# Tile 0's expert sum as products with diagonals of the gates, a new order behind it, and an earlier load of half of v

## The chip, the cores and the metric

The kernel runs on one core of one Trainium2 chip. What counts is the device time of one execution in microseconds (us); for the kernel before it is the median of three runs. A measurement of this kernel repeats within about 0.1%.

## What is computed

Two transformer-like blocks run one behind the other on 512 tokens of width 1024. The change lies at the seam: the end of the first block's mixture of experts, the two norms, and the first product of the second block. Cut to this:

```python
gates = jax.nn.softmax(top_val, axis=-1)              # 4 of 32 experts for each token
y_rows = lax.map(expert_block, (x_blocks, block_e)).reshape(n_rows, d)
y_rows = y_rows * row_gate[:, None]
y = jnp.zeros((n_tok, d), h.dtype).at[row_tok].add(y_rows)
x = x + g2[:, None, :] * y                            # end of the MoE
x = _rmsnorm(x, final_g)                              # end of the first block
h = rms_norm(x, g_norm[l]) * (1.0 + scale[:, None, :]) + shift[:, None, :]
proj = h @ w_in[l]                                    # q, k, v, gates ...
```

So each token's result is the sum of four rows of y_rows, each times a gate; then come a residual, a norm, a second norm, and the product with v's weights.

## The kernel before

Each engine has its own program, and semaphores order them. Tokens lie in TT = 4 tiles of P = 128; the width is KT = 8 slabs of 128. x_t and h_t hold x and h with the width on the partitions.

**The experts.** In NP = 33 passes TensorE multiplies gathered rows by expert weights, which SyncE (SP) loads into 16 slots; the results go by keep_y to y_sb and by store_quarter to y_rows in HBM, in four stores for each pass. Of the last pass ScalarE issues two stores and SP two (lines 476 to 478). Then each engine reads how many spare blocks there are (none in these runs) and passes an empty loop; in it TensorE executes keep_on(1, 3) three times. keep_on(count, bank) (L607 to L610) is filler: `count` products of the identity with a constant of 128x512, whose result nobody reads.

**The gathers.** GpSimd waits until all stores have landed, then issues 16 indirect gathers (L2467) of 128 rows of 4 KB each: parts[:, 4t + k] is the k-th expert's row of each token of tile t. The four of tile 0 signal one by one ("first parts 0" to "first parts 3"), those of tiles 1 to 3 together for each tile.

**Tile by tile.** For tile t VectorE makes add_part(t, 0) to (t, 3): acc = sum of gate times part (L2168 and L2170, 128x1024). TensorE has put the experts' second bias into two PSUM banks (second_bias, L1037), and turn_sum(t) (L1045) adds the transposed sum, 8 matmuls with the identity as moving operand; each signals after its first and its second half ("sum turned"). VectorE adds it to x_t, residual(t) (L2181, 8 operations in two halves), ScalarE squares both halves (L1519), TensorE adds the squares up in norm_sums(t) (L1053), ScalarE takes the root (L1523, for tile 0 behind a load of its function table), VectorE the reciprocal (tile_scale, L2187), TensorE spreads it over the partitions (spread_scale, L1059), VectorE scales (tile_scaled, L2193, 8 operations) and ScalarE shifts (L1528, 8 operations), which gives h. Then v_rows(t, i) (L1071) multiplies h of the tile by half i of v's weights: 8 matmuls of 512 columns. Half i lies in ring[4i + 4 : 4i + 8]; load_v(0) is issued behind the last use of those slots as expert weights, load_v(1) behind the gather of part 3 of tile 0 (L500, L501; the DMA itself is L472). ScalarE keeps the results (keep_v_rows, L1532).

**What sets the order.** It is written out by hand in each engine's program. TensorE: second_bias(0), (1), (2), keep_on(6, 0), turn_sum(0), keep_on(2, 0), norm_sums(0), keep_on(2, 0), spread_scale(0), turn_sum(1), v_rows(0, 0), norm_sums(1), v_rows(0, 1), spread_scale(1), turn_sum(2), v_rows(1, 0), norm_sums(2), v_rows(1, 1) and so on. VectorE: the parts of tile 0, residual(0), three parts of tile 1, tile_scale(0), the fourth, tile_scaled(0), residual(1), tile 2's four parts, three of tile 3, tile_scale(1), the fourth, tile_scaled(1), residual(2), and so on. A matmul of these types stands in the trace as two records, so v_rows has 16, and turn_sum too.

Behind v come 40 pairs of weight slabs (pair_begun, pair_ended, L1112), with attention and a recurrent layer between them.

## Time and profile before

| | us |
|---|---|
| median of 3 runs (lowest, highest) | 1996.19 (1994.83, 1996.49) |
| the profiled execution | 1998.96 |
| its span, first to last instruction | 1997.7 |
| TensorE matmuls busy | 1937.8 |
| VectorE busy | 836.2 |
| ScalarE busy | 424.7 |
| GpSimd busy | 240.0 |

Mean granted TensorE clock: 0.987 of full speed. Times in rows count from the first instruction. PE is TensorE, PEld its weight loads, DVE VectorE, ACT ScalarE, POOL GpSimd; SPq, ACTq and POOLq are DMA issues of SyncE, ScalarE and GpSimd. L12 is line 12 of the kernel. A row of the timeline gives start, duration, engine, line, operation, output and inputs, shape, count, and in brackets the idle time of that engine before it with what ended it; "remote" there means that the profile knows the moment of the release but no instruction to put it to. Rows that are equal and adjacent are merged, with the count behind the x. The ends of matmuls are modelled. "1.00" in a clock column is 2.4 GHz, "0.50" 1.2 GHz.

### The profile page before, as it was taken

To read this page: it belongs to the slowest core of one execution; us is meant where nothing else is said; L and a number is where in the kernel's file an instruction comes from. 1 tells how busy PE (TensorE), PEld (TensorE's weight loads), DVE (VectorE), ACT (ScalarE), POOL (GpSimd) and SP (SyncE) were. 2 spreads that over 40 slices of the span, in tenths; PEclk is the share of its full clock that TensorE was granted. 3 is DMA by queue.
4 is the path that set the end of the run, shared out by engine and by line. 5 is a ranking of instruction groups with operands and counts; after the bars stand their busy time and mean duration, and the time that the engine had idled before them with its cause. 6 is when DMAs were issued, how large, how long until landed. Compare 5 with 4: busy or idle time off the path is not lost.

```text
span 1997.7 us, 38345 instructions
## 1 busy us (share of the span) xinstructions
PE 1937.8 (97%) x16481; PEld 1079.1 (54%) x16481; DVE 836.2 (42%) x1530; ACT 424.7 (21%) x914; POOL 240.0 (12%) x173
## 2 busy tenths in 40 slices
PE   8999998999999999999999999989999999999998
PEld 4455544433434434343443433345588888888887
DVE  5989875211121211121120211105458678654465
ACT  3223512210111110011010111102233443431102
POOL 0000000000000000000000000002244334360011
PEclk8999998999999999999999999998999999999999
DMA  8475796999799999999999999975112112122221
GB/s 339 139 282 195 286 335 268 420 419 366 319 421 419 420 420 419 421 419 420 419 419 420 418 420 416 419 295 225 63 68 89 67 67 89 66 85 85 85 85 64
DMA packets 103419, 553.94 MB, mean 277 GB/s; under 512 B 14224, under 2 KB 25488, under 8 KB 48336
## 3 DMA queue, kind: packets, MB, share of 16 engines
q1 hardware_dynamic: 81344, 516.84, 64.1%
q10 hardware_dynamic: 14848, 17.82, 2.7%
q0 software_dynamic: 7056, 16.79, 2.3%
q8 instruction: 133, 2.18, 0.4%
q14 instruction: 38, 0.31, 0.0%
HBM read 532.91 MB, written 26.35 MB: 280 GB/s over the span
## 4 chain that ended last, share of the span: by engine, by line
PE 72%; DMA 13%; SPq 10%; DVE 3%; issue 2%; ACT 1%; another core or an unknown queue 0%; ACTq 0%; DVEq 0%
PE psum L1112 24%; PE psum L926 19%; DMA arena<-in_w 9%; SPq L467 9%; PE psum L934 9%; PE psum L597 7%; PE psum L1071 3%; DMA ring<-in_w 2%; DMA arena<-in_mod_slabs 1%; PE psum L919 1%; PE psum L1199 1%; PE psum L1218 1%; PE psum L942 1%; PE psum L906 1%; PE psum L781 1%
## 5 line engine op out<-in xcount | busy, mean ns | idle before, releaser
L926 PE MATMUL psum<-arena,ring 128*32 128x512 f32 x4096 | 452.7, 596 | 11.3 <-DMA arena<-in_w 10.8
L926 PEld LDWEIGHTS psum<-arena,ring 128*32 128x32 f32 x4096 | 134.3, 110 | 310.1 <-issue 307.1
L2114 DVE TENSOR_SCALAR h_t<-psum 128x512 f32<-128x512 f32 (+2 forms) x33 | 27.9, 845 | 572.5 <-PE psum L926 572.5
L934 PE MATMUL psum<-arena,h_t 128*32 128x256 f32 x3840 | 217.9, 380 | 4.2 <-DMA arena<-in_w 3.3
L1458 ACT ACTIVATE ring<-psum,mods,gain 128x64 f32<-128x64 f32 (+2 forms) x264 | 85.6, 429 | 607.5 <-PE psum L906 607.5
L934 PEld LDWEIGHTS psum<-arena,h_t 128*32 128x32 f32 x3840 | 120.7, 110 | 101.1 <-issue 18.7
L2435 POOL DMA_INDIRECT ring<-h_rows,row_i x33 | 35.5, 1075 | 1144.0 <-PE psum L906 834.9
L1112 PE MATMUL psum<-ring 128*128 128x256 f32 x768 | 171.1, 379 | 0.0
L1112 PEld LDWEIGHTS psum<-ring 128*128 128x128 f32 x768 | 145.9, 190 | 20.1 <-issue 0.3
L1112 PE MATMUL psum<-h_t,ring 128*128 128x256 f32 x672 | 154.3, 379 | 0.2 <-ACT arena L1532 0.2
L926 PE MATMUL psum<-ring 128*32 128x512 f32 x1344 | 148.8, 593 | 5.5 <-DMA ring<-in_w 5.4
L1112 PEld LDWEIGHTS psum<-h_t,ring 128*128 128x128 f32 x672 | 126.4, 190 | 23.8 <-issue 7.7
L597 PE MATMUL psum<-h_t,ring 128*128 128x512 f32 x256 | 116.8, 611 | 2.5 <-ACT h_t L1278 2.5
L1112 PE MATMUL psum<-arena,ring 128*128 128x256 f32 x544 | 119.1, 379 | 0.0
L1112 PEld LDWEIGHTS psum<-arena,ring 128*128 128x128 f32 x544 | 103.3, 190 | 14.2 <-DVE arena L2268 0.2
L926 PEld LDWEIGHTS psum<-ring 128*32 128x32 f32 x1344 | 44.4, 110 | 103.4 <-issue 103.4
L934 PE MATMUL psum<-ring,h_t 128*32 128x256 f32 x1600 | 90.9, 380 | 3.8 <-DMA ring<-in_w 3.1
L2128 DVE COPY h_t<-psum 128x512 f32<-128x512 f32 (+2 forms) x33 | 27.9, 845 | 154.9 <-PE psum L942 154.9
L597 PEld LDWEIGHTS psum<-h_t,ring 128*128 128x128 f32 x256 | 48.7, 195 | 62.9 <-issue 61.8
L1466 ACT ACTIVATE work<-psum 128x512 f32<-128x512 f32 (+2 forms) x33 | 23.8, 720 | 240.8 <-PE psum L934 240.8
L934 PEld LDWEIGHTS psum<-ring,h_t 128*32 128x32 f32 x1600 | 50.2, 110 | 43.8 <-issue 7.8
L1112 PE MATMUL psum<-work,ring 128*128 128x256 f32 x256 | 60.7, 380 | 1.7 <-DVE work L2268 1.7
(480 smaller groups left out, 2132.6 us busy)
## 6 DMA issues: line engine op xcount, KB each, us to landing
arena<-in_w SPq DMA_DIRECT2D x288, 1024.0 KB, 30.9
ring<-in_w SPq DMA_DIRECT2D x96, 1024.0 KB
ring<-in_pairs SPq DMA_DIRECT2D x40, 1024.0 KB, 4.8
ring<-in_dot_slabs SPq DMA_DIRECT2D x40, 512.0 KB, 5.9
ring<-in_mod_slabs SPq DMA_DIRECT2D x6, 2048.0 KB, 9.2
ring<-in_proj_slabs SPq DMA_DIRECT2D x24, 512.0 KB, 4.4
y_rows<-arena SPq DMA_DIRECT2D x3, 3584.0 KB, 25.0
y_rows<-work ACTq DMA_DIRECT2D x70, 64.0 KB, 7.7
```

The costliest lines, as they stand in the source:

```text
L467: sp.dma_start(slot[s], source).then_inc(sem(f"weights {s} loaded"), 16)
L597: mm = pe.matmul(bank, ring[:, n % 4, k, :], src[:, k, :], start=(k == 0), stop=(k == KT - 1))
L781: mm = pe.matmul(bank, w_glu[:, m, k, :], proj[:, k, :], start=(k == 0), stop=(k == 3))
L926: mm = pe.matmul(psum[32 * j:32 * j + 32, g, :], x_e[:, c * tokens + g * TG:c * tokens + g * TG + TG], slot[s][:, j * S:(j + 1) * S], star ...
L934: mm = pe.matmul(psum[32 * j:32 * j + 32, 6 + g // 2, (g % 2) * 256:(g % 2) * 256 + 256], h_e[:, g * 256 + half * P + 32 * c:g * 256 + hal ...
L1071: mm = pe.matmul(psum[:, 4 + i, :], h_t[:, k, t * P:(t + 1) * P], ring[:, 4 * i + 4:4 * i + 8, k, :], start=(k == 0), stop=(k == KT - 1))
L1112: mm = pe.matmul(out, stationary[:, k, :], moving[:, k, :], start=(start and k == 0), stop=(k == 3), skip_group_check=True)
L1458: act.activation(x_e[:, k * tokens:(k + 1) * tokens], psum[:, 4 + k // 4, (k % 4) * tokens:(k % 4 + 1) * tokens], ACT.Identity, bias=mods[ ...
L1466: act.activation(dst[:, 0:256 * groups], src[:, 0:256 * groups], ACT.Copy).then_inc(sem("y kept"), 1)
L2114: dve.tensor_scalar(gate, psum[:, 0:groups, 0:256], LIMIT, None, ALU.min).then_inc(sem("gate clipped"), 1)
L2128: dve.tensor_copy(h_e[:, 0:256 * groups], src[:, 0:256 * groups]).then_inc(sem("h_e kept"), 1)
L2435: pool.indirect_dma_start(out=x_g[n][0:rows, :], out_offset=None, in_=h_rows, in_offset=bass.IndirectOffsetOnAxis(ap=index, axis=0), bound ...
```

## The change

Tile 0's sum is made on TensorE: VectorE writes four diagonal matrices, identity times the gates of one expert rank, into by_gate (the space of x_g[1], which is free then), and turn_parts multiplies each part by its diagonal as soon as it has been gathered, 32 matmuls that add up in PSUM. The ten filler products around it go. turn_sum(1) moves behind v_rows(0, 0); norm_sums(1) moves into the middle of v_rows(0, 1); VectorE makes tile 1's four parts behind tile_scaled(0); ScalarE keeps v_rows(0, 0) ahead of the squares of tile 1. SP issues load_v(1) directly behind its two stores of the last pass, without the wait for part 3.

```diff
@@ -294,6 +294,7 @@
+        by_gate = x_g[1][:, 0:TOPK * P].rearrange("p (k n) -> p k n", k=TOPK)
@@ -476,6 +477,7 @@
                 store_quarter(sp, NP - 1, j)
+            load_v(1)
@@ -497,8 +499,6 @@
-            sp.wait_ge(sem("first parts 3 gathered"), 16)
-            load_v(1)
@@ -1038,9 +1038,19 @@
+            def turn_parts():
+                a = SUM_AT[0]
+                pe.wait_ge(sem("gates laid out"), TOPK)
+                for part in range(TOPK):
+                    pe.wait_ge(sem(f"first parts {part} gathered"), 16)
+                    for k in range(KT):
+                        mm = pe.matmul(psum[:, a + k // 4, (k % 4) * P:(k % 4 + 1) * P], parts[:, part, k * P:(k + 1) * P], by_gate[:, part, :], start=False, stop=(part == TOPK - 1), skip_group_check=True)
+                        if part == TOPK - 1 and k % 4 == 3:
+                            mm.then_inc(sem("sum turned"), 1)
             def turn_sum(t):
-                pe.wait_ge(sem("parts summed"), t + 1)
+                pe.wait_ge(sem("parts summed"), t)
@@ -1061,7 +1071,7 @@
-            def v_rows(t, i):
+            def v_rows(t, i, between=None):
@@ -1069,6 +1079,8 @@
+                    if between and k == 3:
+                        between()
@@ -1077,16 +1089,12 @@
             second_bias(2)
-            keep_on(6, 0)
-            turn_sum(0)
-            keep_on(2, 0)
+            turn_parts()
             norm_sums(0)
-            keep_on(2, 0)
             spread_scale(0)
+            v_rows(0, 0)
             turn_sum(1)
-            v_rows(0, 0)
-            norm_sums(1)
-            v_rows(0, 1)
+            v_rows(0, 1, lambda: norm_sums(1))
             spread_scale(1)
@@ -1538,8 +1546,8 @@
+            keep_v_rows(0, 0)
             tile_squares(1)
-            keep_v_rows(0, 0)
             tile_root(1)
@@ -2160,9 +2168,7 @@
-                if t == 0:
-                    dve.wait_ge(sem(f"first parts {k} gathered"), 16)
-                elif k == 0:
+                if k == 0:
                     dve.wait_ge(sem(f"parts {t} gathered"), 16 * TOPK)
@@ -2192,14 +2198,14 @@
+            dve.wait_ge(sem("x turned"), NP)
             for k in range(TOPK):
-                add_part(0, k)
+                dve.tensor_scalar(by_gate[:, k, :], identity, gates[:, 0, k:k + 1], None, ALU.mult).then_inc(sem("gates laid out"), 1)
             residual(0)
-            for k in range(3):
+            tile_scale(0)
+            tile_scaled(0)
+            for k in range(TOPK):
                 add_part(1, k)
-            tile_scale(0)
-            add_part(1, 3)
-            tile_scaled(0)
             residual(1)
```

## Rows read from the trace of the kernel before

**Rows 1.** The page's first part: busy us, share of the span, instructions.
```profile
PE 1937.8 (97%) x16481; PEld 1079.1 (54%) x16481; DVE 836.2 (42%) x1530; ACT 424.7 (21%) x914; POOL 240.0 (12%) x173
```

**Rows 2.** The chain that ended last, 1330 to 1450 us: start, duration, what.
```profile
1369.27 3.78 PE psum L1045 x16
1373.05 8.14 PE psum L1071 x16
...
1382.87 6.97 PE psum L1071 x16
...
1389.95 1.79 PE psum L1045 x16
...
1398.61 1.68 PE psum L1053 x16
...
1427.59 13.99 PE psum L1071 x32
```

**Rows 3.** Windows: busy us (instructions) of each engine, granted clock, DMA share, GB/s.
```profile
1345.00:1350.00 5.00, 5.00 (x51) 4.22 (x51) 0.82 (x1) 0.00 (x0) 3.78 (x5) 1.00 0.72 225
...
1360.00:1365.00 5.00, 3.27 (x14) 2.66 (x15) 2.99 (x6) 1.91 (x2) 3.78 (x5) 0.68 1.02 415
...
1375.00:1380.00 5.00, 5.00 (x12) 2.13 (x11) 4.89 (x5) 0.00 (x0) 0.00 (x0) 0.95 0.45 184
```

**Rows 4.** DMA queues (packets, MB, share): 1356 to 1357; 1360 to 1365; 1350 to 1355.
```profile
q1 hardware_dynamic: 9, 0.04, 12.7%
...
q1 hardware_dynamic: 265, 1.08, 52.6%
q0 software_dynamic: 276, 1.00, 49.5%
...
q0 software_dynamic: 450, 1.63, 93.8%
```

**Rows 5.** Timeline, from the last stores of y to tile 0's turned sum.
```profile
1339.89 1.81 SPq L350 DMA_DIRECT2D y_rows<-work  x2
...
1344.60 0.95 POOL L2467 DMA_INDIRECT arena<-y_rows,slot_i  x1 [115.15 <-DMA y_rows<-work]
...
1354.47 0.41 SPq L472 DMA_DIRECT2D ring<-in_v_slabs  x1
1354.54 1.28 DVE L2170 SCALAR_TENSOR_TENSOR arena<-arena,cols 128x1024 f32<-128x1024 f32 x1 [0.27 <-issue]
...
1355.88 2.05 PE L1045 MATMUL psum<-consts,arena 128*128 128x128 f32 x16 [1.42 <-issue]
```

**Rows 6.** Timeline, from there to the scale of tile 0.
```profile
1357.77 1.89 PE L610 MATMUL psum<-consts 128*128 128x512 f32 x4
...
1360.33 1.13 DVE L2181 SCALAR_TENSOR_TENSOR x_t<-psum,mods,x_t 128x128 f32<-128x128 f32 x4 [1.75 <-remote]
...
1362.14 1.28 ACT L1523 ACT_TABLE_LOAD   x1
...
1362.17 1.86 PE L1053 MATMUL psum<-par,h_t 128*128 128x2 f32 x8 [1.74 <-ACT h_t L1519]
...
1363.90 3.76 PE L610 MATMUL psum<-consts 128*128 128x512 f32 x4
...
1367.50 0.26 ACT L1523 ACTIVATE par<-psum,consts 128x1 f32<-128x1 f32 x1 [4.08 <-remote]
...
1368.08 0.48 PE L1059 MATMUL psum<-consts,par 128*128 128x128 f32 x1 [0.42 <-DVE par L2187]
```

**Rows 7.** Timeline: releases by matmuls of tiles 1 and 2, and the one of L886.
```profile
1373.09 1.13 DVE L2181 SCALAR_TENSOR_TENSOR x_t<-psum,mods,x_t 128x128 f32<-128x128 f32 x4 [0.58 <-PE psum L1045]
...
1400.32 0.26 ACT L1523 ACTIVATE par<-psum,consts 128x1 f32<-128x1 f32 x1 [1.08 <-PE psum L1053]
...
317.44 0.23 DVE L2027 COPY work<-psum 128x64 f32<-128x64 f32 x1 [0.86 <-PE psum L886]
```

**Rows 8.** Timeline: three multiply-adds of tile 2.
```profile
1374.91 3.92 DVE L2170 SCALAR_TENSOR_TENSOR arena<-arena,cols 128x1024 f32<-128x1024 f32 x3
```

## The prediction

> **What bounds the kernel now.** I read the page first: TensorE is busy 97% of the span [rows 1], so a change pays only where it takes time out of TensorE's own row or closes one of its holes. The diff touches one stretch, between the last expert product (1339 us) and the first paired product (1442 us). The second view is the chain of waits in that stretch [rows 2]. From 1369.27 us on the chain is TensorE without a hole worth naming: turn_sum(1), v_rows(0, 0), norm_sums(1), v_rows(0, 1) and so on to v_rows(3, 1), whose last group ends at 1441.6 us. What follows (40 pairs of slabs) is on TensorE too. So whatever brings v_rows(0, 0) forward from 1373.05 us arrives at the end of the kernel, less what is put into the dense part behind it.
>
> Before 1369 us the chain is the path of tile 0, and TensorE waits in it. The timeline [rows 5, 6] shows: the last stores of y are issued at 1339.9 to 1341.7, the first gather at 1344.60, and the fourth part of tile 0 is there at about 1354.4 (the second half of v's slabs, which waits for it, is issued at 1354.47). VectorE multiplies in part 3 (1.28 us), TensorE turns the sum (2.05 us), then come residual, squares, norm_sums, root, spread, scaling. Two steps of this take far longer than their instructions. The second half of the sum has left TensorE at 1357.93, yet the residual that waits for it starts at 1360.33; norm_sums ends at 1364.03, yet the root that waits for it starts at 1367.50. The profile names no releaser ("remote") for either. Both times the matmuls directly behind the one that signals are those of keep_on, the filler products: 1357.77 to 1359.66 and 1363.90 to 1367.66 [rows 6].
>
> The windows [rows 3] add two facts. The granted clock falls within 1360 to 1365 (mean 0.68), in spite of the filler, from 2.4 to 1.2 GHz; in 1375 to 1380 the mean is 0.95, so it is back at about 1375.5. And the DMA engines are full in the window at 1360 (share 1.02), but not in the one at 1345 (0.72).
>
> **The change part by part.** *The v load moved up.* On SP's queue it goes from behind the wait for part 3 (1354.47) to directly behind the two stores of y, so to 1341.75 [rows 5]. Nothing waits behind it on SP but scalar work; ScalarE's and SP's stores are already issued. Its first packets came about 2.0 us after its issue (9 packets in 1356 to 1357) [rows 4], so now at 1343.75, which is 0.85 us ahead of the first gather; that gather waits for the stores to land, and SP's stores stand ahead of the load in its queue: I take no cost there, and 0.5 us as the upper end. Its 2.1 MB run alone until the gathers' packets start (1346.2, 1.6 us behind their issue), which, at the 415 GB/s of full engines [rows 3] is 1.0 MB. The other 1.1 MB share the engines: while both queues ran, v's had 1.08 MB and the gathers 1.00 MB in 5 us [rows 4]. That is 5 us to 1351.2, with 0.95 MB of gathers done. Four parts are 2.1 MB; the rest goes at the rate of the gathers alone, 1.63 MB in 5 us, so 3.5 us, and about 1.1 us lie between last byte and release as before (four parts' bytes were over at 1353.2 by the same rates, the release was at 1354.4): 1355.8 instead of 1354.4. Cost 1.4 us at the head (bounds: 0.5, if the idle engines take nearly all of v; 2.5, if v goes wholly first). The gathers of tiles 1 to 3 gain, as v no longer runs beside them; they are off the path. The old place covered nothing: v_rows(0, 1) starts at 1382.9, and is now reached at about 1375, 24 us behind v's last byte.
>
> *The sum of tile 0 on TensorE.* Four multiply-adds on VectorE go (of them 1.28 us behind the last part count). Four products with diagonals of the gates come (128x128; the nearest row has four such operations in 1.13 us [rows 6]; VectorE does them while it waits for the first part, and would have to be 1 us late for them to show; nothing). TensorE does 32 matmuls instead of 8: 1.79 to 2.05 us per part [rows 2, 5]. The parts come every 1.3 to 2 us, so it falls behind: 1350.5, 1353.1, 1355.0 and, for part 3, 1356.9 as start. That is 1.0 us later than turn_sum(0) starts now (1355.88). So this edit alone wins nothing at the head; it pays through DVE's queue later.
>
> *keep_on gone.* I expect the two late releases to go with it. Against 1.75 and 4.08 us of idle "remote" [rows 6] stand releases of the same kinds where no filler follows: the second half of the residual of tile 1 starts at 1373.09, 0.04 us after turn_sum(1)'s last record, and the root of tile 2 at 1400.32, as soon behind norm_sums(2) [rows 2, 7]. One row speaks against: the matmul of L886 is followed by keep_on(4, 3), and VectorE, which waited for it, starts at 317.44, with L886 named as releaser [rows 7]. I cannot name the mechanism, so both ends stay: nothing is left of the stalls, or all of it.
>
> *Tile 0 from the start of part 3's products.* First half of the residual ends at +2.25, second at +3.4 (1.13 us each); square and start of the table load +0.7; table load 1.28 (norm_sums's second half, 0.95 to 1.86 us, lies beside it); root 0.3; its end to the end of spread_scale 0.8; scaling and shift of the first slab 0.8 (the first waits 0.3 behind spread_scale, each takes 0.3 to 0.4) [rows 6]. Together 7.5 us: v_rows(0, 0) starts at 1364.4, against 1373.05: **minus 8.7 us**. The Trainium skill (ScalarE: Activation LUTs, What ACT_TABLE_LOAD costs) adds a drain of about 1.38 us to each switch of tables; by it the sum would be 1.4 us worse. The trace shows the load taking 1.28 us and nothing that must be a drain, so I leave it out.
>
> *Order behind it.* turn_sum(1) now stands behind v_rows(0, 0): **plus 1.8** [rows 2]. VectorE sums tile 1 behind tile_scaled(0), 7 us after that begins, which v_rows(0, 0) (6.9 us, more at the lower clock) hides; if it ran at full clock at once, 0.3 us would show. norm_sums(1) between k = 3 and 4 is free: its squares are ready 1.5 us before. keep_v_rows(0, 0) ahead of tile_squares(1) is free as well.
>
> *A new wait.* tile_scale(1) still stands behind add_part(2, 0 to 3) and add_part(3, 0 to 2). From the start of turn_sum(1): residual(1) ends at +3.3, tile 2 costs 0.75 + 3.92 [rows 8], three parts of tile 3 3.4, the reciprocal 0.1: +11.5. TensorE arrives at spread_scale(1) at 1.79 + 6.97 + 1.68 = +10.45 [rows 2]. **Plus 1.1**; then h of tile 1 is 0.1 late for v_rows(1, 0). Now this is covered, since the sums run while TensorE is still in v_rows(0, 0).
>
> *Clock.* Before, v_rows(0, 0) took 8.14 us instead of 6.87: 1.27 lost behind its start [rows 2]. Dense work began at 1369.27 and the clock returned at 1375.5, 6.2 us later [rows 2, 3]. Now the thin stretch ahead is as long (about 1358.8 to 1364.4), so the clock is again low at the start of v_rows(0, 0). If it stays so for the same 6.2 us, half of that, 3.1, is lost (plus 1.8); if for half as long, 1.6 (plus 0.3). The nearer row is the first, but dense work now begins with v_rows itself and not with a turn_sum; I take 5.2 us: 2.6 lost, **plus 1.3**.
>
> Sum: -8.7 + 1.8 + 1.2 + 1.3 = **-4.4 us**. The profiled execution (1998.96, its span 1997.7) would come to 1994.6; its median of runs is 1996.19, so 1991.8. The forecast's own range, from the terms' bounds (head -0.9 to +1.1, clock -1.0 to +0.5, the wait at spread_scale(1) to either side by 0.5), is 1990.2 to 1993.6.
>
> **Rivals.**
> A, *late releases stay* (slower): if they belong to the full DMA engines of that stretch and not to the filler, the root is again 6.1 us late (1367.50 against 1355.88 + 5.5). -4.4 + 6.1 = +1.7: 1997.9. For it: the engines are full [rows 3] and the keep_on behind L886 is harmless [rows 7]. Against: turn_sum(1) at 1369 to 1373 releases on time [rows 7], while the gathers still run. It is slower than before once more than 4.4 of the 6.1 us remain.
> B, *the clock falls inside the part products*: between second_bias and part 0, and between parts, TensorE has nothing to do, where six fillers stood. At the lower clock 16 records take 3.78 us [rows 2] instead of 2.05 [rows 5]; two parts slow cost about 3 us: 1994.8. Against: the window 1345 to 1350 stays at 1.00 [rows 3], though its first 4 us hold only second_bias. The Trainium skill (TensorE: Matmul & The Clock Gate, Part 1) has an idle array fall to half clock, which speaks against taking the filler out. By that the trace agrees only in part: the clock fell with the filler in place too [rows 3].
> C, *the v load hurts the head more*: stores of y late and v ahead of all gathers, +1.6 us: 1993.4.
> D, *more is won*: v fills only idle time and the clock returns early: 1989.8.
>
> **How the numbers follow.** Forecast 0.56, A 0.14, B 0.11, C 0.10, D 0.09. A measurement of this kernel tells about 0.2% (4.0 us) from no change, so "faster" is below 1992.2: D and rather more than half of the forecast's range, 0.44; "slower" (over 2000.2) needs A with B or C (0.03) or something that no row shows (0.04), 0.07; the rest, 0.49, is "same". The range 1989.2 to 1997.5 leaves out the worst half of A and the best of D.
>
> **What would show it.** Right: turn_parts's last products start near 1357; residual(0) and root(0) are released within 0.1 us of their matmuls; v_rows(0, 0) starts near 1364.4; one idle place of about 1 us ahead of spread_scale(1), ended by VectorE; low clock until 1367 to 1371; v's packets over by 1351.5. Wrong: "remote" waits at those two lines again (A), the granted clock at 0.50 before 1358 (B), the first gather later than 1344.8 or part 3 later than 1356.5 (C). It would also be wrong if tile 2's or 3's parts held VectorE.

## The result and the profile after

The changed kernel takes 2004.58 us (median of 11 runs, 2001.69 to 2009.9). The kernel before, in 11 runs beside it, takes 1996.87 (1991.22 to 2002.37). The ratio is 1.0036, 95% interval 1.0024 to 1.0048: about 7 us slower (7.7 by the medians), where 4.4 us faster was forecast. The profiled execution (2001.69, span 2000.4) is the shortest of the eleven, so the traces understate the difference: its span is only 2.7 us longer than that of before.

| | us |
|---|---|
| the profiled execution | 2001.69 |
| its span | 2000.4 |
| TensorE matmuls busy | 1935.2 |
| VectorE busy | 832.6 |
| mean granted clock | 0.986 |

TensorE has 2.6 us less to do than in [rows 1], so the time went into holes:

```profile
PE 1935.2 (97%) x16509; PEld 1084.0 (54%) x16509; DVE 832.6 (42%) x1530; ACT 424.8 (21%) x914; POOL 238.5 (12%) x173
```

The moment of the first gather differs from execution to execution, from 1336.35 to 1344.60 us over all traces of this study. What it depends on isn't known. So from here on stages are counted from the issue of the first gather; in before that is 1344.60 [rows 5], in after 1338.97. The timeline of after, the columns as in [rows 5]; L1037 is second_bias, L1047 turn_parts, L2187 residual, L1063 norm_sums, L1531 the root, L1069 spread_scale, L1081 v_rows, L1055 turn_sum, L2193 tile_scale:

```profile
1338.97 0.95 POOL L2473 DMA_INDIRECT arena<-y_rows,slot_i  x1 [115.14 <-DMA y_rows<-work]
1340.17 7.17 PE L1037 MATMUL psum<-work,ring 32*128 32x128 f32 x48
...
1347.27 5.51 PE L1047 MATMUL psum<-ring,arena 128*128 128x128 f32 x28
...
1354.53 0.27 PE L1047 MATMUL psum<-ring,arena 128*128 128x128 f32 x1 [0.93 <-issue]
...
1355.93 0.49 PE L1047 MATMUL psum<-ring,arena 128*128 128x128 f32 x2 [1.12 <-issue]
...
1358.05 0.27 PE L1047 MATMUL psum<-ring,arena 128*128 128x128 f32 x1 [1.64 <-issue]
...
1360.88 0.37 PE L1047 MATMUL psum<-ring,arena 128*128 128x128 f32 x1 [1.54 <-issue]
1361.58 4.98 PE L1047 MATMUL psum<-ring,arena 128*128 128x128 f32 x27 [0.33 <-issue]
1365.70 2.16 DVE L2187 SCALAR_TENSOR_TENSOR x_t<-psum,mods,x_t 128x128 f32<-128x128 f32 x8 [35.78 <-PE psum L1047]
...
1370.30 0.26 ACT L1531 ACTIVATE par<-psum,consts 128x1 f32<-128x1 f32 x1 [0.47 <-PE psum L1063]
...
1372.25 8.79 PE L1081 MATMUL psum<-ring,h_t 128*128 128x512 f32 x16 [0.96 <-ACT h_t L1536]
...
1380.87 1.95 PE L1055 MATMUL psum<-consts,arena 128*128 128x128 f32 x16
...
1392.08 0.16 DVE L2193 RECIPROCAL par<-par 128x1 f32<-128x1 f32 x1
...
1392.30 0.32 PE L1069 MATMUL psum<-consts,par 128*128 128x128 f32 x1 [0.82 <-DVE par L2193]
```

Three things stand in it. The bias takes 7.17 us. The 64 records of the products fall apart: between 1352.8 and 1361.6 TensorE executes nine of them and is idle between them with no wait, only "issue" behind the arrow, seven holes of 0.31 to 1.64 us, 6.3 us in all. And on this trace the waits by which the two late releases of before were seen (1.75 and 4.08 us "remote" [rows 6]) are gone: residual and root each start 0.2 us or less behind the matmul that signals.

The windows of after (columns as in [rows 3]):

```profile
1345.00:1350.00 5.00, 5.00 (x30) 4.78 (x28) 0.00 (x0) 0.00 (x0) 3.75 (x4) 0.50 1.03 409
1350.00:1355.00 5.00, 3.56 (x21) 3.19 (x20) 0.00 (x0) 0.00 (x0) 3.74 (x4) 0.83 1.02 407
1355.00:1360.00 5.00, 1.32 (x4) 1.06 (x5) 0.00 (x0) 0.00 (x0) 2.81 (x3) 0.86 1.03 410
1360.00:1365.00 5.00, 3.79 (x18) 3.71 (x18) 0.00 (x0) 0.00 (x0) 0.00 (x0) 0.50 0.72 288
```

The clock is at 1.2 GHz while the bias and the first products run, then at 2.4 GHz through most of the holes, then at 1.2 GHz again. In the window at 1355 TensorE is busy 1.32 of 5 us beside full DMA engines. It can't be waiting for a part: the packets of tile 0's four gathers were over 10.0 us behind the first gather, the holes lie at 13.8 to 22.6 us, and six of the seven stand inside a part, three of these between the two records of one matmul, where the program has no wait. Nor is late loading of instructions to be seen: the instruction queue (q8) moved one packet at 1.8 us and one at 10.8 us, 1.0 us each, as in e6 below (2.0 and 11.0), which has no holes.

One thing is missing from this trace. Behind a gather's rows come 16 packets of 4 bytes, which update its semaphore (256 such packets for the sixteen gathers in every trace, and 256 updates in e6), and from the updates the profile tells when it landed. In its list of DMA issues the gathers of e6 have a median time from issue to landing, those of after none (e6 first, then after):

```profile
arena<-y_rows,slot_i POOLq DMA_INDIRECT x16, 7.3
```

```profile
arena<-y_rows,slot_i POOLq DMA_INDIRECT x16
```

All packets are there in both traces, but many updates are not in that of after: from 4 to 22 us behind the first gather it has 219 such packets and 48 updates, from 22 us on 37 and 38. That stretch takes in the holes and begins some 10 us ahead of them. So "issue" and "remote" are weak words there: the profile can't name a releaser that wasn't recorded.

The stages of all traces, in us behind the first gather. Each time is that at which a record starts: "bias" and "products" (turn_sum(0) or turn_parts) are first to last record, "end of v" is the last record of v_rows(3, 1), 556.6 to 557.2 us ahead of the end of the span in every trace. A record's own length comes on top: the products of e6 start their last record at 17.6 and end at 17.9 us.

| trace | kernel before in the same measurement | bias | products | v_rows(0, 0) | end of v | from v_rows(0, 0) to the end of v |
|---|---|---|---|---|---|---|
| before | | 0.6-4.2 | 11.3-13.1 | 28.2 | 96.4 | 68.1 |
| after | 1996.87 | 1.2-8.0 | 8.3-27.3 | 33.3 | 104.8 | 71.5 |
| e5, before | 1991.14 | 2.4-9.1 | 17.5-19.1 | 27.3 | 94.2 | 66.8 |
| e10, before | 1989.59 | 2.0-8.7 | 17.1-18.8 | 27.0 | 93.8 | 66.8 |
| e6, after | 1991.14 | 0.8-7.6 | 7.9-17.6 | 23.6 | 95.0 | 71.5 |
| e9, after | 1989.59 | 2.2-9.0 | 9.3-19.1 | 25.0 | 96.6 | 71.6 |
| e15, after | 1989.98 | 0.3-6.4 | 7.1-15.7 | 21.0 | 93.9 | 72.9 |
| e17, after | 1996.95 | 0.2-6.6 | 7.5-24.7 | 30.9 | 102.6 | 71.7 |
| e1 | 1991.03 | 1.7-5.6 | 12.6-14.4 | 22.9 | 89.7 | 66.8 |
| e2, late load | 1991.03 | 2.0-8.7 | 9.1-18.9 | 24.7 | 96.3 | 71.6 |
| e4, other queue | 1991.03 | 0.2-5.2 | 8.2-18.2 | 23.6 | 95.1 | 71.5 |
| e12, entry filler | 1989.98 | 0.8-10.8 | 11.1-20.9 | 26.8 | 98.4 | 71.6 |
| e14, products, entry filler | 1989.98 | 0.8-12.0 | 12.3-21.1 | 29.3 | 96.1 | 66.8 |
| e13 | 1989.98 | 0.6-7.1 | 15.0-16.7 | 24.9 | 91.7 | 66.8 |
| e16, order alone | 1996.95 | 0.6-6.9 | 14.3-15.9 | 31.2 | 102.7 | 71.5 |
| e8, products alone | 1991.14 | 1.2-7.9 | 15.8-22.8 | 31.0 | 97.8 | 66.8 |
| e7, with filler | 1991.14 | 1.7-8.4 | 16.2-23.2 | 29.8 | 99.6 | 69.8 |
| e3, held | 1991.03 | 1.1-7.8 | 8.2-17.6 | 22.9 | 96.6 | 73.7 |
| e11, held | 1989.59 | 1.7-5.4 | 7.3-16.0 | 22.0 | 98.3 | 76.3 |
| e18, held | 1997.24 | 2.0-8.8 | 9.1-18.8 | 24.8 | 100.9 | 76.1 |

The last column goes by the order of instructions: 66.8 us in the old one (68.1 in before, whose clock is low at v_rows(0, 0)), 71.5 to 71.7 in the new one (72.9 in e15, 69.8 in e7, where the clock is full at v_rows(0, 0)), more where gathers are held. The products' column is where the chips differ. The measurements fell on several chips, and the second column sorts them: on three of them (e1 to e15) the kernel before takes 1989.6 to 1991.1 us, on two others (e16 and e17; e18) and in the first measurement, whose chip isn't known, 1996.9 to 1997.2. I call the latter the 1997 chips. So the kernel's time repeats within 0.1% on one chip (1991.03 and 1989.59 on that of e1 and of e9), but chips differ by 0.4%. The traces of the 1997 chips alone lack updates: in the 50 us behind the first gather they hold 124 (after), 125 (e17), 143 (e16), 192 (e18) and 195 (before) by DMA, all others 301 to 304.

### The profile page after: what moved, and what is told of

Its sections match the earlier page's. It is cut to its first block, busy times and chain, and to the rows that moved or that the text cites. A ratio compares the mean times of both kernels' runs of the same rounds, so it can differ in the third digit from the quotient of the medians.

```text
span 2000.4 us, 38398 instructions
## 1 busy us (share of the span) xinstructions
PE 1935.2 (97%) x16509; PEld 1084.0 (54%) x16509; DVE 832.6 (42%) x1530; ACT 424.8 (21%) x914; POOL 238.5 (12%) x173
## 4 chain that ended last, share of the span: by engine, by line
PE 68%; DMA 14%; SPq 13%; DVE 3%; issue 2%; ACT 1%; ACTq 0%; DVEq 0%
PE psum L1120 24%; PE psum L926 16%; SPq L468 12%; DMA arena<-in_w 9%; PE psum L597 7%; PE psum L934 7%; DMA ring<-in_w 3%; PE psum L1081 3%; DMA arena<-in_mod_slabs 1%; PE psum L1207 1%; PE psum L1226 1%; PE psum L919 1%; PE psum L781 1%; PE psum L1212 1%; PE psum L1047 1%
## 5 line engine op out<-in xcount | busy, mean ns | idle before, releaser
L926 PE MATMUL psum<-arena,ring 128*32 128x512 f32 x4096 | 450.4, 593 | 12.8 <-DMA arena<-in_w 12.2
L934 PEld LDWEIGHTS psum<-arena,h_t 128*32 128x32 f32 x3840 | 120.8, 110 | 100.8 <-issue 17.9
## 6 DMA issues: line engine op xcount, KB each, us to landing
arena<-in_w SPq DMA_DIRECT2D x288, 1024.0 KB, 30.9
ring<-in_w SPq DMA_DIRECT2D x96, 1024.0 KB, 30.9
```

The lines of the kernel that those rows point to most:

```text
L926: mm = pe.matmul(psum[32 * j:32 * j + 32, g, :], x_e[:, c * tokens + g * TG:c * tokens + g * TG + TG], slot[s][:, j * S:(j + 1) * S], star ...
L934: mm = pe.matmul(psum[32 * j:32 * j + 32, 6 + g // 2, (g % 2) * 256:(g % 2) * 256 + 256], h_e[:, g * 256 + half * P + 32 * c:g * 256 + hal ...
```

## The experiments

**e1 to e4: early load alone; products with a late load; held gathers; another queue.** The question: which part costs, and do the gathers of tiles 1 to 3 disturb TensorE? e1 is the kernel before with load_v(1) behind the stores. e2 is the changed kernel with load_v(1) at its old place. The edit of e1, and of e3 in the changed kernel:

```diff
+            load_v(1)
...
-            sp.wait_ge(sem("first parts 3 gathered"), 16)
-            load_v(1)
```

```diff
             for n in range(TT * TOPK):
+                if n == TOPK:
+                    pool.wait_ge(sem("sum turned"), 2)
```

e4 leaves out the gathers of tiles 1 to 3 and lets SyncE load consecutive rows of the same size in their place, behind the same waits for the stores. Its output isn't the reference's; it is there for its trace:

```diff
...
+            for n in range(TOPK, TT * TOPK):
+                sp.dma_start(parts[:, n, :], y_rows[n * P:(n + 1) * P, :]).then_inc(sem(f"parts {n // TOPK} gathered"), 16)
...
-            for n in range(TT * TOPK):
+            for n in range(TOPK):
```

> The kernel before with one edit: load_v(1) directly behind the last stores of y. Measure: from the issue of the first gather to the start of v_rows(0, 0) it was 28.45 us in the kernel before and 33.3 us in the changed one. Theory V (the early load of v is what hurts): about half or more of the 4.8 us appears here, 31 to 33 us, and the time is 3 us or more above that of before. Theory G (TensorE completes its instructions slowly while the gathers' traffic runs, and the change puts 32 matmuls of tile 0's path into that stretch): the load costs the head 0.6 to 1.4 us and frees the later gathers, so 28 to 30 us and a time within 2 us of before.

> The changed kernel with load_v(1) back in its old place behind the fourth part. Theory V: the stretch from first gather to v_rows(0, 0) falls to 28 to 29 us, and the time to that of before or below. Theory G: the products still run beside the gathers, TensorE shows gaps of 0.7 to 1.9 us between matmuls that wait for nothing, and the stretch stays at 31 to 35 us, the time 5 to 9 us above before.

> The changed kernel, but GpSimd issues the gathers of tiles 1 to 3 only when tile 0's sum has been turned (semaphore sum turned at 2). Theory G: the gaps inside the 32 products go, part 3's products end about 2 us after part 3 lands, some 12 us after the first gather instead of 27.6, and v_rows(0, 0) starts 18 to 20 us after the first gather; then tile 1's parts are late (4 gathers, about 8 us after the sum) but hidden or nearly so by v_rows(0, 0). The time is 4 to 10 us below the changed kernel. Theory C (the low clock, since the filler is gone, is what makes the products slow): the gaps stay, the stretch stays over 28 us and the time as that of the changed kernel or more.

> The changed kernel, but the rows of tiles 1 to 3 come as 12 plain copies of the same size issued by SyncE from consecutive rows of y_rows; the gathers of tiles 1 to 3 are left out. The DMA engines are as full, but only 4 gathers are issued by GpSimd. Theory G1 (full DMA engines slow TensorE, whichever queue feeds them): gaps between the products as in the changed kernel, 8 us or more lost in them. Theory G2 (it is the gathers by GpSimd's queue, not the traffic as such): no gaps behind the fourth gather, part 3's products end 10 to 14 us after the first gather.

Measured, beside the kernel before at 1991.03: e1 1990.47, ratio 0.9999 (0.9988 to 1.0011); e2 1991.04, 1.0002 (0.9987 to 1.0017); e3 1994.64, 1.0023 (1.0009 to 1.0036); e4 1992.67 in one execution. None of these four traces has a hole between products or a late release, with the gathers beside them or not. So they could not tell what makes the holes. They do show that the early load alone is worth nothing, to within 0.1%, and that the products with the new order (e2) are level with before where there are no holes. Holding the gathers costs time: tile 1's parts come late, and from v_rows(0, 1) to v_rows(1, 0) 12.9 us pass instead of 11.6.

**e5 to e8: both kernels again, with filler, products alone.** e5 and e6 are the kernels before and after, unchanged. e7 puts the ten fillers back into the changed kernel (keep_on(6, 0) ahead of turn_parts, twice keep_on(2, 0)). e8 has the products, the early load and the fillers, but the old order behind them.

```diff
             second_bias(2)
+            keep_on(6, 0)
             turn_parts()
+            keep_on(2, 0)
             norm_sums(0)
+            keep_on(2, 0)
             spread_scale(0)
```

> The kernel before, unchanged, for a second trace. Measure from here on: from the issue of the first gather to the last record of v_rows (96.4 us in the kernel before as first traced, 104.8 in the changed one, 89.7 in the kernel before with the early load of v). Theory S (the late releases are not the filler's but come in some executions, whatever the kernel): here 89 to 92 us, no remote wait, and a ratio of 1.000. Theory K (the filler makes them): remote waits of 1.75 and 4 us again, and 95 to 97 us.

> The changed kernel, unchanged, for a second trace. Theory S: no gaps between the 32 products, 95 to 98 us in the stretch, and a time 3 to 7 us over before. Theory G (the gathers' traffic always opens the gaps where both the early load and the products are there): gaps of 0.7 us and more again, 103 to 106 us, and 7 to 12 us over before.

> The changed kernel with the ten filler products back in their old places: keep_on(6, 0) ahead of the part products, keep_on(2, 0) behind them and behind norm_sums(0). Theory C (without filler the granted clock stays at its lower level through second_bias and most of the 32 products, about 13 us, and this is 2 to 4 us of the loss): the clock is back within 9 us of the first gather and high at the start of v_rows(0, 0); products start 2.6 us later but take 7 to 8 us instead of 9.4; the stretch is 1 to 3 us shorter than that of the changed kernel in this call. Rival (order is all): stretch as in the changed kernel or 1 to 2 us longer, as the filler stands in front of the products.

> The early load of v and tile 0's sum as products, with all filler and with the old order behind it (turn_sum(1) ahead of v_rows(0, 0), norm_sums(1) between the two, three parts of tile 1 ahead of tile_scale(0)). Theory C and O together (products cost through the clock and TensorE's queue, the new order costs 4 to 5 us behind v_rows(0, 0)): the order's share is gone, from v_rows(0, 0) to v_rows(1, 0) it takes 17.4 to 19 us instead of 22.1, and the stretch is 90 to 94 us. Rival (the products alone are the loss): the stretch stays over 95 us.

Measured, beside 1991.14: e5 1.0004 (0.9993 to 1.0015), e6 1.0001 (0.9992 to 1.0011), e7 1996.74, 1.0016 (1.0005 to 1.0027), e8 1995.2, 1.0023 (1.0012 to 1.0034). So the changed kernel, unchanged, is level with before on this chip. Its timeline in e6 against that of after above:

```profile
1338.20 0.96 POOL L2473 DMA_INDIRECT arena<-y_rows,slot_i  x1 [115.19 <-DMA y_rows<-work]
1339.01 7.17 PE L1037 MATMUL psum<-work,ring 32*128 32x128 f32 x48
1346.11 9.95 PE L1047 MATMUL psum<-ring,arena 128*128 128x128 f32 x64
...
1361.79 8.76 PE L1081 MATMUL psum<-ring,h_t 128*128 128x512 f32 x16 [0.97 <-ACT h_t L1536]
...
1370.38 1.95 PE L1055 MATMUL psum<-consts,arena 128*128 128x128 f32 x16
...
1381.81 0.32 PE L1069 MATMUL psum<-consts,par 128*128 128x128 f32 x1 [0.83 <-DVE par L2193]
```

One row of 64 records without a hole stands where after has 19 us of pieces. Behind it every duration is that of after, to 0.03 us. Filler in front of the products is harmful: in the timeline of e8 it runs mostly at the low clock and takes 7.64 us. The products behind it then run at full clock, 7.30 instead of 9.95 us, but the filler didn't bring that clock sooner: it rises 12.8 us behind the first gather in e8 and 13.3 us in e6, without filler:

```profile
1346.42 7.64 PE L610 MATMUL psum<-consts 128*128 128x512 f32 x12
1353.90 7.30 PE L1047 MATMUL psum<-ring,arena 128*128 128x128 f32 x64
```

What filler does hold is the clock behind the products. In e7, with the new order, v_rows(0, 0) runs at full clock:

```profile
1369.09 7.11 PE L1081 MATMUL psum<-ring,h_t 128*128 128x512 f32 x16 [0.96 <-ACT h_t L1539]
```

**e9 to e11: the same once more, on a third occasion.** The kernels after and before, and e3's kernel.

> The changed kernel a third time, to see on which runs TensorE's gaps appear. As first traced it has 9 us of gaps inside the 32 products and 104.8 us from the first gather to the end of v_rows; in the second trace none and 95.0 us. Theory S (a property of the chip or moment, which hits what stands in the gathers' stretch): where the gaps are there, 103 to 106 us and 5 to 9 us over before; where not, 94 to 97 us and within 2 us of before. Theory G (always): 103 to 106 us.

> The kernel before a third time, a trace beside e9_after_third. Theory S: remote waits exactly if e9_after_third has gaps; then 95 to 97 us in the stretch, else 89 to 94.5 us, as the clock falls out.

> The changed kernel with the gathers of tiles 1 to 3 held until tile 0's sum is turned, beside e9_after_third. If e9_after_third has gaps: theory G1 (the gathers' traffic opens them) has them end within 3 us of part 3's landing, and the stretch 4 to 9 us shorter than in e9_after_third; theory H (something outside the core opens them) has them in the products all the same. If e9_after_third has none: 96 to 97 us, 1 to 2 us more than e9_after_third, from the wait for tile 2's and 3's parts.

Measured, beside 1989.59: e9 1992.89, 1.0013 (1.0002 to 1.0025); e10 1993.1 in one execution; e11 1998.94, 1.0042 (1.0030 to 1.0053). No holes, no late release. e10 is the kernel before with its fillers, and this timeline of it is to be read beside [rows 5, 6]. It has no late release; and its clock is low at the entry, so that keep_on(6, 0) takes 8.19 us:

```profile
1350.39 8.19 PE L610 MATMUL psum<-consts 128*128 128x512 f32 x12
1358.42 1.95 PE L1045 MATMUL psum<-consts,arena 128*128 128x128 f32 x16
1359.51 2.16 DVE L2181 SCALAR_TENSOR_TENSOR x_t<-psum,mods,x_t 128x128 f32<-128x128 f32 x8 [6.48 <-PE psum L1045]
1360.20 1.88 PE L610 MATMUL psum<-consts 128*128 128x512 f32 x4
...
1363.62 1.96 PE L610 MATMUL psum<-consts 128*128 128x512 f32 x4
1363.80 0.26 ACT L1523 ACTIVATE par<-psum,consts 128x1 f32<-128x1 f32 x1 [0.17 <-PE psum L1053]
```

Fillers stand directly behind both signalling matmuls, and both releases are on time. So filler behind the signalling matmul isn't enough to make a release late. e11 shows in passing that the bias can hide something: there it is over 5.7 us behind the first gather, and the products wait 1.60 us for part 0:

```profile
1349.74 9.01 PE L1047 MATMUL psum<-ring,arena 128*128 128x128 f32 x64 [1.60 <-DMA arena<-y_rows,slot_i]
```

**e12 to e15: a warmer entry.** If the low clock at the head is the rest of the loss, filler ahead of the bias (keep_on(4, 3) behind the last expert product, in e12 and e14 also keep_on(1, 0) between the three calls of second_bias) should give it back. e12 is the changed kernel with it, e13 is e1 with keep_on(4, 3) there, e14 the products with the old order and such filler in place of keep_on(6, 0), e15 the changed kernel as it is. The edit of e12:

```diff
+            keep_on(4, 3)
...
             second_bias(0)
+            keep_on(1, 0)
             second_bias(1)
+            keep_on(1, 0)
             second_bias(2)
```

> The changed kernel with six filler products where TensorE waits anyway: keep_on(4, 3) behind the last expert product, ahead of the empty loop, and one each between second_bias(0), (1) and (2). Theory C (low clock through bias and products is what ate the head's gain: v_rows(0, 0) starts 23.6 to 25 us after the first gather where 19.8 was forecast): the clock is high through bias and products, products start at 6 to 7 us and end at 14 to 15, v_rows(0, 0) starts at 20 to 21 us, the stretch is 90 to 92 us, and the time 3 to 5 us below the changed kernel, 1 to 4 below before. Rival (the filler only delays): clock low all the same, products end at 18 us or later, stretch 95 us or more.

> The kernel before with the early load of v and with keep_on(4, 3) behind the last expert product; all its other filler stays. Theory C: clock high, sum of tile 0 turned at 12.5 to 14.5 us, v_rows(0, 0) at 22.5 to 23.5 us, stretch 89 to 90.5 us instead of 93.8 to 94.2, time 2 to 4 us below before. Rival: low clock, stretch 93 to 95 us, time as before.

> Early load of v, products with the gates' diagonals, the old order behind them, entry filler as in e12_after_entry instead of keep_on(6, 0). If the theories of clock and order both hold, this is the best of them: v_rows(0, 0) at 21 to 22.5 us, then 66.8 us as in the old order: stretch 88 to 89.5 us, time 3 to 6 us below before. If the order is not the loss behind v_rows(0, 0), it stays over 91 us.

> The changed kernel a fourth time, one look. Gaps inside the products and 103 to 106 us if the chip is of the kind of the first trace, else none and 94 to 97 us.

Measured, beside 1989.98: e12 1991.88, 1.0017 (1.0003 to 1.0032); e13 1989.44, 1.0002 (0.9993 to 1.0012); e14 1992.95, 1.0009 (0.9996 to 1.0022); e15 1993.52 in one execution. The filler shifts the low clock instead of removing it: in e12 it is low from 6.5 to 16.7 us and from 23.5 to 30.4 us behind the first gather, the bias takes 10 us with the fillers between, and the products, at 11.1 to 21.2 us, run their first 5.6 us at the low clock all the same (10.05 us, as in e6). None beats the kernel before by more than its interval.

**e16 and e17: order alone, and after beside it.** e16 is the kernel before with the early load and the new order on all engines, but with VectorE's sum of tile 0 and the fillers.

> The kernel before with the early load of v and the new order of all engines (turn_sum(1) behind v_rows(0, 0), norm_sums(1) inside v_rows(0, 1), tile 1's parts behind tile_scaled(0)), but with VectorE's sum of tile 0 and the ten fillers kept. Theory 'the order gives back what the products win': v_rows(0, 0) begins one turn_sum earlier than with the early load alone, but from its start to the end of v about 71.5 us pass instead of 66.8; together +1 to +3 us against the kernel before, ratio 1.0005 to 1.0015, and one wait of VectorE's release of about 1 us ahead of spread_scale(1). Theory 'the products are at fault': without them the order costs nothing, 66.8 us behind the start of v_rows(0, 0), ratio 0.998 to 1.000.

> The changed kernel once more, beside the one above and the kernel before. If the 9 us of holes between the 32 products belong to the chip or the moment of the first measurement, none here: products over about 10 us behind their first, ratio 1.000 to 1.0015. If they belong to the kernel in some of its executions: holes of several us between products and 1.003 again.

This measurement fell on a 1997 chip. Measured, beside 1996.95: e16 1999.04, 1.0006 (0.9994 to 1.0018); e17 2003.62, 1.0036 (1.0023 to 1.0049). e16's ratio is the one that was expected of the order, though 1 lies in its interval. e17 is the first result again, and its timeline has the holes again, of up to 2.33 us:

```profile
1348.48 7.16 PE L1047 MATMUL psum<-ring,arena 128*128 128x128 f32 x48 [0.56 <-issue]
...
1357.91 0.50 PE L1047 MATMUL psum<-ring,arena 128*128 128x128 f32 x3 [2.27 <-issue]
...
1360.74 0.60 PE L1047 MATMUL psum<-ring,arena 128*128 128x128 f32 x2 [2.33 <-issue]
...
1362.87 0.37 PE L1047 MATMUL psum<-ring,arena 128*128 128x128 f32 x1 [1.53 <-issue]
1363.58 2.49 PE L1047 MATMUL psum<-ring,arena 128*128 128x128 f32 x10 [0.34 <-issue]
```

The first of these holes stands ahead of part 3, whose packets were over at 10.1 us; the others lie inside it. e16, on the same chip and without products, shows the late releases of before, now of both halves of turn_sum(0):

```profile
1357.84 1.95 PE L1044 MATMUL psum<-consts,arena 128*128 128x128 f32 x16
...
1361.31 1.13 DVE L2181 SCALAR_TENSOR_TENSOR x_t<-psum,mods,x_t 128x128 f32<-128x128 f32 x4 [4.51 <-PE psum L1044]
...
1366.27 1.13 DVE L2181 SCALAR_TENSOR_TENSOR x_t<-psum,mods,x_t 128x128 f32<-128x128 f32 x4 [3.83 <-remote]
```

The second half left TensorE at 1359.79 and is released 6.5 us later. The four traces of 1997 chips with free gathers (the chip of before and after counted among them by its times and its missing updates) agree on when it ends: the last hole or late release is over 22.6 us (after, 1361.58), 22.6 (e17, 1363.58), 22.7 (e16, 1366.27) and 22.9 us (before, 1367.50 [rows 6]) behind the first gather. They begin at 13 to 15 us. Behind the start of v_rows(0, 0) the order alone takes 71.5 us instead of 66.8, of which 1.8 us are turn_sum(1), moved there from the head. So the theory that the products are at fault for that part falls.

**e18: gathers held, on a 1997 chip.** e3's kernel once more.

> The changed kernel with the 12 gathers of tiles 1 to 3 held back until tile 0's sum has been turned. It speaks only if this chip is one of those on which the kernel before takes about 1997 us. Theory 'the gathers of tiles 1 to 3 make TensorE's holes': products end by 18 us behind the first gather with no hole over 1 us, and the first v_rows begins at about 23 us instead of 31 to 33. Theory 'the holes belong to TensorE's own program on that chip, whatever the DMA engines do': holes of 1 to 2.5 us between products as before, first v_rows at 28 us or later. On a chip with the kernel before near 1990 us: no holes in either, 22 to 23 us, and 0.2 to 0.4% slower than the kernel before as the late parts hold up tiles 1 to 3.

It fell on a second 1997 chip. Measured, beside 1997.24: 1999.72, ratio 1.0007 (0.9988 to 1.0025), where the changed kernel with free gathers has 1.0036 twice. The timeline of e18, then its window at 1355:

```profile
1343.16 7.17 PE L1037 MATMUL psum<-work,ring 32*128 32x128 f32 x48
...
1350.26 9.97 PE L1047 MATMUL psum<-ring,arena 128*128 128x128 f32 x64
1359.38 2.16 DVE L2187 SCALAR_TENSOR_TENSOR x_t<-psum,mods,x_t 128x128 f32<-128x128 f32 x8 [27.31 <-PE psum L1047]
```

```profile
1355.00:1360.00 5.00, 5.00 (x44) 5.00 (x43) 0.62 (x3) 0.00 (x0) 0.00 (x0) 0.93 0.00 0
```

With no traffic beside them the products run in one piece, as on the other chips: v_rows(0, 0) starts at 24.8 us instead of 30.9 and 33.3. The changed kernel loses its holes when the gathers of tiles 1 to 3 are taken away, and gives 4.6 us of it back through late parts (76.1 us behind v_rows(0, 0) instead of 71.5).

e18's chip is not e17's, but it is of the same kind, and not by the level of the kernel before alone. e18's trace lacks updates of the held gathers, as those with free gathers do: from 22 to 36 us it has 112 of their packets and 29 updates, from 36 us on 80 and 79. Those of tile 0's gathers, which ran ahead of the hold, are complete. And in that stretch of missing updates one release is late again. residual(1) waits for the first half of turn_sum(1) and starts 3.0 us behind the start of turn_sum(1); in e11, with the same program on another chip, it is 1.2 us. Behind the record that signals it is 1.8 us, and 0.04 us in every other trace of the new order (e18, then e11):

```profile
1374.66 2.05 PE L1055 MATMUL psum<-consts,arena 128*128 128x128 f32 x16
...
1377.64 2.16 DVE L2187 SCALAR_TENSOR_TENSOR x_t<-psum,mods,x_t 128x128 f32<-128x128 f32 x8 [3.04 <-PE psum L1055]
```

```profile
1373.18 2.05 PE L1055 MATMUL psum<-consts,arena 128*128 128x128 f32 x16
...
1374.38 2.16 DVE L2187 SCALAR_TENSOR_TENSOR x_t<-psum,mods,x_t 128x128 f32<-128x128 f32 x8 [1.25 <-PE psum L1055]
```

No filler stands behind turn_sum(1) here. So the disturbance moved with the gathers, from 13 to 23 us to 36.5 us behind the first one. It ends before their traffic does: in the five traces of 1997 chips the last hole or late release is over 3.1 to 3.9 us behind GpSimd's issue of the last gather (18.7 to 19.8 us, in e18 33.2), at about the time from which the updates are complete again, while packets run on until 26.0 to 30.9 us, in e18 until 43.7.

## Why the prediction was wrong

**Head, forecast -8.7 us.** This is the step that failed. v_rows(0, 0) was forecast at 19.8 us behind the first gather (1364.4 less 1344.60), where before has 28.2; it starts at 33.3, so the head became 5.1 us longer instead of 8.7 shorter. Of the 13.5 us between forecast and trace, 3.8 are there in e6 too, where nothing stalls (23.6; it would be 1.2 in e15 and 5.2 in e9), and the other 9.7 are not. Three parts of the working failed.

The first is the term for the products, which took 1.79 to 2.05 us a part, and the bias, which was taken as it stood in before. The end of the products was forecast at 14.4 us. In e6, without holes, they end at 17.9 and v_rows(0, 0) starts at 23.6, so the path from the products on was right (5.7 us against 5.4, although the terms that the prediction lists for it add up to 7.3 us and not to 7.5), and 3.5 us are lost up to there: 7.17 us of bias and 9.95 us of products at a clock that is low from before the first gather to 13 us behind it. Rival B priced this nearly right, at 3 us, and its chance of 0.11 was low, but its cause was another: it had the clock fall because the six fillers are gone. The clock is low before the bias starts, with filler behind it (e5, e10) and without: at the entry it is at 1.2 GHz in after, e2, e3, e5 to e10 and e18, and the one trace on which B was judged, where the window at 1345 stands at 1.00 [rows 3], is not the common case. One trace gives one draw of the clock: e1's is a lucky one (89.7 us to the end of v), and its median is that of before all the same.

The second is the starting point. Before's head was read as 28.2 us from the first gather, of which 5.8 us (1.75 and 4.08) were two late releases that the change was to end. On the chips without them the head is 27.0 to 27.3, because there the clock is low at the entry and the fillers themselves run late (8.19 us for keep_on(6, 0) in e10). The gain over these is 2 to 6 us (21.0 to 25.0 in e6, e9, e15), not 8.7.

The third, and on the 1997 chips the largest, is the products' length in the gathers' stretch, which had no term for a stall at all. The products span 19.0 us in after and 17.2 in e17 from first to last record, against 9.7 in e6. 6.3 and 6.5 us of that are holes; another 1.9 us in after are its last 27 records, which run at the lower clock (4.98 us, by the 7.30 us for 64 records of e8 3.1 at full clock).

**"I expect the two late releases to go with it."** Wrong in its cause. The fillers aren't needed for it: e10 has them and is on time, e18 has a late release without them, and after and e17 have none and are hit harder. What disturbs TensorE on 1997 chips was seen from about 13 to 22.9 us behind the first gather; before had turn_sum(0), norm_sums(0) and filler in that stretch and lost some 6 us of waits, the change puts 64 records there and loses 7.5 (e17) to 9.3 us (after, against e6). Rival A had the right suspicion, "the full DMA engines of that stretch", but let the stall stand where it had been, with nothing on the products, and so gave +1.7 us in place of +7. Its "against", that turn_sum(1) releases on time while the gathers run, was weak: 1373.09 is 28.5 us behind the first gather, when packets still ran (until 30.9) but the last gather had been issued 8.7 us before.

**Order behind v_rows(0, 0), forecast +4.3 us in its three terms (1.8, 1.1 with 0.1, 1.3).** Right in kind, and the clock's term too dear. From v_rows(0, 0) to the end of v before takes 68.1 us in the first trace and after 71.5, +3.4, which is the number to set beside the forecast; against the traces of before at full clock, 66.8, it is +4.7. At full clock on both sides (e7 against e5) it is 69.8 less 66.8, +3.0. The terms: turn_sum(1) 1.8 (1.95 in the row); spread_scale(1) waits 0.82 us for VectorE, forecast 1.1, with TensorE elsewhere dense; v_rows(0, 0) takes 8.76 to 8.79 us against 7.03 at full clock, 1.7 lost. The forecast was 2.6 lost against 1.27 in before, so this term is some +0.5 and not +1.3. norm_sums(1) inside v_rows(0, 1) is free, as said.

**Load of v, forecast +1.4.** Too dear. It fills the engines ahead of the gathers, as said (DMA queues of after, 1340 to 1342 us):

```profile
q1 hardware_dynamic: 197, 0.81, 98.8%
```

Part 0 lands 7.4 us behind the first gather in e6, against 4.1 in e5, and part 3 at 11.2 against 10.6. Yet the products wait for no part: in e6 all 64 records stand in the row that starts with the end of the bias. The low clock of the bias hid what the load costs; in e11, with the clock up in the bias, 1.60 us of it shows. e1, with the load alone, is at 0.9999.

**The sum, then.** Where TensorE isn't disturbed: -3.4 at the head and +4.7 behind it (e6 against e10), measured 0.0 to 0.13% slower. On a 1997 chip: 102.6 and 104.8 against 96.4 us to the end of v, +6 to +8 us, measured +7.2 (0.36% of 1997). The range, 1989.2 to 1997.5, did not reach 2004.58, because no case let the stall grow with the number of matmuls put into the stretch. (The bounds that the prediction lists for its own terms add up to 1989.4 to 1993.9, not to 1990.2 to 1993.6; that changes nothing here.)

**What stays open.** How the gathers slow TensorE, and why on some chips only. Semaphore updates are missing from the traces in the same stretches on the same chips. Whether one thing delays TensorE and loses the records, or whether the recording itself takes part in the delay, no run here tells: every timed execution has a measured span and clock, so the times aren't free of it either. Full DMA engines alone are not enough: in the expert stage of e17 they are as full, at 1.02, and TensorE has no such holes (window 900 to 1000):

```profile
900.00:1000.00 100.00, 100.00 (x1173) 39.24 (x1166) 16.21 (x19) 12.08 (x30) 3.42 (x3) 1.00 1.02 420
```

There the traffic is weights from SyncE's queue, here GpSimd's indirect gathers, and the end of the disturbance goes by their issue rather than by their packets, which is a hint and not a test. A kernel with plain loads in place of gathers on a 1997 chip would tell these apart; e4 is that kernel, but ran on another chip.

## What to carry to other kernels

Work that is moved to TensorE because it "only waits there" also moves into whatever disturbs TensorE at that place: count how many of its instructions fall into the disturbed stretch, and give the forecast one case in which a stall seen in the trace grows with them. Before a stall is put to the instruction beside it, look for the same pair where it is harmless, in more than one execution and if possible on more than one chip. And a shorter head is worth only what the order behind it doesn't take back: here -3.4 against +4.7 us.

## What was not expected of the hardware

The same kernel takes 1989.6 to 1991.1 us on three chips and 1997.0 and 1997.2 on two others, at nearly the same mean granted clock (0.991 and 0.988). In the stretch of the gathers the traces from the 1997 chips show matmuls that are issued 0.3 to 2.3 us late with no wait, or finished and released up to 6.5 us late, until 22.6 to 22.9 us behind the first gather each time. With the gathers of tiles 1 to 3 held back the products show none of it, and one late release stands beside the held gathers instead. The same traces lack a part of the semaphore updates of these gathers.

The clock stood at 1.2 GHz for the first 16 us of a stretch of TensorE without a hole, in which the last keep_on of the empty loop, second_bias and keep_on(6, 0) run (e10, 1339.60 to 1356.0; this is one window of it, with second_bias alone):

```profile
1345.00:1350.00 5.00, 5.00 (x40) 5.00 (x39) 1.84 (x2) 0.00 (x0) 3.83 (x4) 0.50 0.95 311
```

The Trainium skill (TensorE: Matmul & The Clock Gate, Part 1) has an idle array fall to half clock. By that the traces agree where filler is left out: in e6 the clock falls a second time, 20 to 27 us behind the first gather, and v_rows(0, 0) takes 8.76 us, while in e8 and e10, with filler, it doesn't. Filler was no surety: in before and e16 it stood in place, and the clock fell all the same, at 17.2 and 21.0 us, where late releases left TensorE idle in spite of it (1.74 and 3.91 us ahead of the second half of norm_sums(0)). And the filler's own time at the head cost more than the clock gave back (e7, 1.0016).
